# Attention's q, k, v projection with tokens on the partitions, in a two-layer trunk on one core

## What is computed

```python
qkv = (xn @ w_qkv).reshape(B, S, 3, N_HEADS, HEAD_DIM).astype(jnp.float32)   # 512 tokens, 16 heads of 64
q = rmsnorm(qkv[:, :, 0], g_q)          # mean square over the 64 channels of a head, per token
k = rmsnorm(qkv[:, :, 1], g_k)
v = qkv[:, :, 2]
for window, dil in DILATED_PAIRS:       # (128,1), (512,4), (2048,16), merged by their denominators
    o, m, den = dilated_branch(q, k, v, rel_table, window, dil)
...
return o.reshape(B, S, D).astype(xn.dtype) @ w_o
```

## Time and profile before

| | |
|---|---|
| median of three runs | 1132.68 us |
| the profiled execution, and its span | 1132.44 us, 1130.6 us |
| granted TensorE clock, mean | 1.000 |
| busy: PE, DVE, ACT, POOL | 99%, 51%, 43%, 41% |
| attention's stages, first matmul to the last | 504.15 to 711.47 us |
| its tail, to the last head's outputs | 711.47 to 741.62 us |

### The profile page before, as it was taken

One profiled execution on the slowest core, in us unless ns is written; L12 is line 12 of the kernel. 1 busy time (PEld: TensorE's weight loads), 2 busy tenths in 40 slices (PEclk: granted clock), 3 DMA queues, 4 the chain that ended last, 5 costly groups with the idle time before them and its releaser, 6 DMA issues.

```text
span 1130.6 us, 16046 instructions
## 1 busy us (share of the span) xinstructions
PE 1124.8 (99%) x5228; PEld 936.7 (83%) x5228; DVE 582.0 (51%) x1047; ACT 487.7 (43%) x750; POOL 461.7 (41%) x221
## 2 busy tenths in 40 slices
PE   9999999999999999999999999999999999999998
PEld 7788888888888888888888888878888888888887
DVE  6875754545445412225777777777844545450000
ACT  5333444444444432324666666644534444341220
POOL 4454534354443445443223332134544344434442
PEclk9999999999999999999999999999999999999999
DMA  8232322322322233332322223122332222223331
GB/s 267 83 106 93 112 77 95 107 93 93 110 78 92 63 108 98 102 109 70 92 75 74 74 88 100 64 75 93 112 111 90 96 95 90 95 63 104 100 100 76
DMA packets 38925, 108.11 MB, mean 96 GB/s; under 512 B 4272, under 2 KB 7344, under 8 KB 38896
## 3 DMA queue, kind: packets, MB, share of 16 engines
q1 hardware_dynamic: 36560, 103.49, 28.7%
q10 hardware_dynamic: 2336, 4.24, 1.3%
HBM read 105.57 MB, written 2.15 MB: 95 GB/s over the span
## 4 chain that ended last, share of the span: by engine, by line
issue 45%; PE 33%; POOL 20%; DMA 1%; POOLq 0%; SPq 0%; ACT 0%; DVE 0%; DVEq 0%
POOL wl L431 20%; PE bank L1087 7%; PE bank L1086 7%; PE bank L1085 7%; PE spt L1085 4%; PE spt L1086 4%; PE spt L1087 4%; DMA raw<-w_in 1%; SPq L361 0%; POOLq L430 0%; POOLq L436 0%; PE obank L1087 0%; PE obank L1086 0%; PE obank L1085 0%; SPq L368 0%
## 5 line engine op out<-in xcount | busy, mean ns | idle before, releaser
L431 POOL TENSOR_TENSOR wl<-raw,wh 128x1024 fp32r<-128x1024 f32 (+2 forms) x214 | 457.5, 2144 | 644.2 <-ACT wh L466 644.2
L1085 PE MATMUL bank<-xh,wh 128*128 128x512 f32 x992 | 390.5, 394 | 0.0
L1087 PE MATMUL bank<-xh,wl 128*128 128x512 f32 x992 | 386.6, 390 | 0.0
L1086 PE MATMUL bank<-xl,wh 128*128 128x512 f32 x992 | 386.2, 389 | 0.0
L466 ACT ACTIVATE wh<-raw 128x1024 fp32r<-128x1024 f32 (+2 forms) x214 | 201.3, 945 | 145.1 <-PE spt L1087 139.4
L1087 PEld LDWEIGHTS bank<-xh,wl 128*128 128x128 f32 x992 | 186.2, 188 | 39.2
L1086 PEld LDWEIGHTS bank<-xl,wh 128*128 128x128 f32 x992 | 186.4, 188 | 37.4
L1085 PEld LDWEIGHTS bank<-xh,wh 128*128 128x128 f32 x992 | 186.3, 188 | 37.2 <-issue 0.4
L908 DVE TENSOR_TENSOR work<-bank,rstd 128x512 f32<-128x512 f32 x88 | 60.6, 691 | 225.0 <-PE bank L1087 223.1
L1085 PE MATMUL spt<-bh,wh 128*128 128x512 f32 x440 | 171.5, 390 | 0.4 <-POOL wl L431 0.3
L1086 PE MATMUL spt<-bl,wh 128*128 128x512 f32 x440 | 171.2, 389 | 0.0
(11 more groups left out here) (155 smaller groups left out, 938.3 us busy)
## 6 DMA issues: line engine op xcount, KB each, us to landing
raw<-w_up SPq DMA_DIRECT2D x88, 512.0 KB, 3.2
raw<-w_down SPq DMA_DIRECT2D x32, 384.0 KB, 3.1
raw<-w_down SPq DMA_DIRECT2D x32, 320.0 KB, 2.9
raw<-w_qkv SPq DMA_DIRECT2D x16, 512.0 KB, 3.6
raw<-w_in SPq DMA_DIRECT2D x14, 512.0 KB, 4.2
raw<-w_out SPq DMA_DIRECT2D x8, 512.0 KB, 3.2
raw<-w_qkv SPq DMA_DIRECT2D x16, 256.0 KB, 2.8
work<-bias_rows ACTq DMA_DIRECT2D x16, 256.0 KB, 3.1
```

Source lines behind the costliest of these rows:

```text
L431: nc.gpsimd.tensor_tensor(wl[s][:, 0:n], raw[s][:, 0:n], plain(wh[s][:, 0:n]), ALU.subtract).then_inc(s_lo, 1)
L1085: mm(dst, wh[s][:, w], hi, start=first, stop=False)
L1086: mm(dst, wh[s][:, w], lo, start=False, stop=False)
L1087: return mm(dst, wl[s][:, w], hi, start=False, stop=last)
```

## The change

The activations become stationary and the weights move. A pair's q, k and v come out together, tokens on the partitions, in blocks of 128 tokens: `token_product` writes 384 columns (128 of each of q, k, v). Four blocks of tokens by 8 slices of channels by three matmuls make 96 matmuls of 384 columns where there were 72 of 512. They go in two passes over the weights, blocks 0 and 1, then 2 and 3, and use banks 0 and 1 both times (pair 0: banks 0 to 3). A unit holds two slices of channels (768 columns, QKV = 4 x 768), and is released in the second pass.

ScalarE takes each block out of PSUM in three operations (`evacuate`); VectorE adds up squares along the free dimension (`sums`), makes the factors (`norm_factors`, twelve linked small operations), and multiplies q and k by them in place (`normalise`). v needs no turning. Instead q and k are turned, 4 transposes each (`turn`), into banks 2 and 3, from where ScalarE rounds them and VectorE takes the rests. The norm's factor of x isn't spread any more (it scales v by token, and cancels in q's and k's norm up to the epsilon, which is scaled). All stages are unrolled, the first activation of ScalarE (to load its table early) is gone, and the tail is in another order.

TensorE and the units:

```diff
-QKV = (SLOT, SLOT, SLOT // 2, SLOT // 2)
+QKV = (6 * P,) * RING
...
-            def qkv_part(p, which, s, k0, k1, at=0):
-                for k in range(k0, k1):
-                    last = product(bank[which][:], s, k - at, xh[:, k, :], xl[:, k, :], k == 0, k == KT - 1)
...
+            def token_product(b, t, k):
+                dst = bank[b][:, 0:3 * P].rearrange("q (w n) -> q w n", w=3)
+                rows = slice(t * P, (t + 1) * P)
+                mm(dst, xh[:, k, rows], pair_weights(wh, k), start=k == 0, stop=False)
+                mm(dst, xh[:, k, rows], pair_weights(wl, k), start=False, stop=False)
+                return mm(dst, xl[:, k, rows], pair_weights(wh, k), start=False, stop=k == KT - 1)
...
+            def turn(pair, which):
+                if which:
+                    pe.wait_ge(s_kn, pair + 1)
+                    pe.wait_ge(s_kl, 2 * pair)
+                else:
+                    pe.wait_ge(s_qn, pair + 1)
+                    pe.wait_ge(s_ql, 2 * pair)
...
+                for t in range(TB):
+                    at = t * 2 * P + which * P
+                    last = nc.tensor.transpose((qbank, kbank)[which][:, t * P:(t + 1) * P],
+                                               qk[pair % 2][:, at:at + P], ident)
...
+            def stage(p):
+                mid, old = p >= 1, p >= 2
+                if old:
+                    score_blocks(p - 2, 1)
+                tokens(p, 0, 0, 5)
+                if mid:
+                    turn(p - 1, 1)
+                tokens(p, 0, 5, 6)
+                if old:
+                    transposes(2 * (p - 2) + 1)
+                tokens_end(p, 0)
+                if p == 0:
+                    norm_stats(2)
+                if mid:
+                    turn(p - 1, 0)
+                if old:
+                    outputs(p - 2, 1)
+                tokens(p, 1, 0, 2)
+                if mid:
+                    score_blocks(p - 1, 0)
+                tokens(p, 1, 2, 6)
+                if mid:
+                    transposes(2 * (p - 1))
+                tokens_end(p, 1)
+                if mid:
+                    outputs(p - 1, 0)
```

TensorE's tail:

```diff
-            wo_part(0, 0, 5)
-            transposes(2 * end - 1)
-            wo_part(0, 5, 6)
-            wo_part(1, 0, 3)
-            score_blocks(2 * end, 0, 1)
-            outputs(end - 1, 1, 0)
-            turn_v(end)
...
+            score_blocks(end - 1, 1)
+            pe.wait_ge(s_vl, TB * PAIRS)
+            wo_part(0, 0, 6)
+            wo_part(1, 0, 3)
+            turn(end, 1)
+            transposes(2 * end - 1)
+            wo_part(1, 3, 5)
+            outputs(end - 1, 1)
+            turn(end, 0)
+            wo_part(1, 5, 6)
+            pe.wait_ge(s_kept, 2)
+            for n in range(2):
+                wo_part(n, 6, 7)
+            score_blocks(end, 0)
```

ScalarE:

```diff
+            def evacuate(pair, t):
...
+                nc.scalar.activation(qk[pair % 2][:, at], bank[b][:, 0:2 * P], ACT.Copy).then_inc(s_qc, 1)
+                if pair:
+                    act.wait_ge(s_kn, pair)
+                nc.scalar.activation(qksq[:, at], bank[b][:, 0:2 * P], ACT.Square).then_inc(s_qs, 1)
...
+                nc.scalar.activation(v_heads(pair, t, lo=False), v_part(b), ACT.Copy,
+                                     scale=small[:, 3, t:t + 1]).then_inc(s_vh, 1)
```

VectorE:

```diff
+            def normalise(pair, which):
+                dve.wait_ge(s_qc, (pair + 1) * TB)
+                view = heads_of(qk[pair % 2], which)
+                nc.vector.tensor_tensor(view, view, factors(1, which), ALU.mult).then_inc((s_qn, s_kn)[which], 1)
...
```

## The result

The changed kernel takes 1167.27 us (median of 4, 1166.44 to 1169.62), the kernel before 1132.63 us on the same chip: ratio 1.031, interval 1.0298 to 1.0323. It is slower by 34.6 us. The forecast was 1162, with 1150 to 1170 as the likeliest case's range and 1122 to 1169 as the range of 80%.

A forecast was written before the change was run, and what follows sets the result against it. TensorE was taken to bind (busy 99%), with each head's chain hidden before. Stages +17.2 us and tail +12.4 gave +29.6 on 1132.44: 1162 us, likeliest case's range 1150 to 1170, range of 80% 1122 to 1169.

The forecast's parts named there:

- likeliest case: GpSimd's units delay divisions and norm factors in the stages, and the tail waits: 1162 us, chance .42.
- TensorE alone: Attention stages counted by TensorE's work without waits: net -2.2 us per pair, stage 24.65 us, eight pairs 17.6 us less.
- the forecast's own terms: TensorE's work per pair: 3.15 us of operations gone, .94 added for two turns, .06 more for the matmuls.
- The norm's block: GpSimd's unit 3 holds the norm factors in each steady stage; TensorE waits 1.25 us before turn k.
- The tail: End of the attention: waits summing to 11.7 us, 5.4 of them for head 13's output; 42.6 us, +12.4.
- signs of being wrong: Divisions at 1.27 us for four, TensorE idle under 1 us per stage, matmuls .19 apart, or granted clock under 1.
- the rival with the clock: TensorE's matmuls at 1.2 instead of 2.4 GHz, +.227 us per 512-column matmul; 1165 to 1175, chance .09 shared with weight loads.
- One block only: In the stages GpSimd gets two units in one go or misses one: stage about 27.9 us, 1150, chance .14.
- Order of issue: Four queued divisions go ahead of GpSimd's unit, only norm factors are held: stage 26.15 us, 1136, chance .09.
- TensorE bound throughout: No waits in stages, the tail's waits gone too: -18.6 us, 1114, chance .08.
- Free chain: Head's chain in the stages stays clear of GpSimd: stage 24.85 us, -6.9, 1125, chance .18.
- Weight loads as the bound: A 188 ns load must end before the next starts: 1.7 us per stage, up to +13.5; chance .09 shared with clock.

The follow-up runs named there:

- e1: Changed kernel, with GpSimd's unit 1 waiting from pair 1 on until VectorE's four divisions of head 0 are done: 1138.63 us, ratio to before 1.0056.
- e3: Kernel before the change, with ScalarE rounding the next pair's weight unit 0 ahead of its copy of v: 1138.32 us, ratio 1.0052.
- e2: As e1, and GpSimd takes unit 3 only behind the norm factors as well: 1133.32 us, ratio 1.0009.
- e6: Changed kernel with both gates on GpSimd and the tail's new order, w_o's units also waiting for divisions of heads 13 and 15: 1121.4 us, ratio .9902.
- e5: Changed kernel without gates, only the tail reordered (q turned behind k, w_o's slice kept earlier, last scores before the previous head's outputs): 1157.77 us, ratio 1.022.
- e7: As e6, and ScalarE rounds pair 0's last unit before loading the exponential's table: 1120.16 us, ratio .9892.
- e8: Changed kernel without gates, with ScalarE rounding units 1 and 2 behind the rounding of the transposed probabilities: 1155.34 us, ratio 1.0188.

## Why the prediction was right, point by point

- **Direction, place and mechanism: right.** GpSimd's two units fall into the four divisions. The forecast had TensorE lose 3.6 us there per stage; the transposes take 3.2 longer, of which 2.5 are idle. e1 shows the cause by taking it away, e3 by bringing it into the kernel before.
- **TensorE alone: nearly right.** Without waits a stage is 25.28 us by e2 and 25.26 by e6; forecast 24.65, though the forecast's own terms (3.15 - .94 - .06) give 24.73. About half of the difference is the pace, .1735 against the .1705 misread in the score block, 96 x .003 = .29 us; for the rest I had counted the slow first matmul behind each removed group as saved, while the new order has as many changes between groups. That this is all of it isn't shown. Over eight stages the saving is 207.3 - 193.6 = 13.7 us (e6, with 2.1 us of waits in its stages), not 17.6.
- **The norm's block: the right place, too large.** L772 is held for 1.72 us (forecast 1.8), but the wait before turn k is 3.4 us in six stages: 1.31 in the first, .3 to .5 in the others, not 1.25. In the stage shown VectorE ended its factors 4.7 us after the stage's end rather than 5.1, and TensorE came to turn k at 6.7 rather than 6.38.
- **The tail: right.** The wait for head 13's output is 5.36 us (forecast 5.4), the tail 43.05 (42.6). e5 shows that it is of the order.
- **What was left out: the clock.** A fall was only a rival, tied to the tail's wait, and a granted clock under 1 stood among the signs of being wrong; it was .990. It fell behind the waits in five of the seven stages too: 28.85 us a stage at full clock, 30.4 otherwise. The step that failed is the sum's assumption that a wait of 1.2 us costs 1.2 us. In the stages, 47 matmuls of 384 columns start mostly .32 us apart instead of .174, 7 us together, and the six behind the wait of 5.4 us take 2.70 (752.41 to 755.11) instead of 1.36. These 8 us are more than the 5.3 between forecast and result; TensorE's own work (+.6 a stage) and smaller waits (about -.4 and, before turn k, -.8 a stage) together make a stage at full clock .65 us shorter than forecast (28.85 against 29.5). So 1162 lies this close to 1167 partly by luck, by two errors of opposite sign, and the measured time is also inside the 1165 to 1175 that the rival with the clock was given.
- **The rivals.** One block only, 1150: out, the four divisions take 4.40 to 5.48 us in all seven stages. Order of issue, with all queued divisions first: out by e3. TensorE bound throughout: out by the waits. Free chain, 1125: out for this kernel, though e6 and e7 reach that state with gates and another tail, 1121 and 1120; its point of decision (a rounding more than about .6 us later) was too simple, for in e8 rounding comes much later and the units then hold up the norm. Weight loads as the bound: out, .1735 is under .188. Of such a lock the Trainium skill ("SBUF — State Buffer", section "Who interferes with whom") says: "Whoever issues first gets the shared pair for the whole instruction". That a held instruction waits for a whole one of the other engine, the trace shows (the second division 2.05 us, .41 alone). But the sentence is about one instruction; that four queued divisions would all go first was my reading of it, and e3 and this trace show GpSimd getting in between them.

## What to carry to other kernels

An engine that is idle half of the time can still set the pace: look at when it asks for something shared, not at how busy it is. A change that takes an instruction out of a third engine's queue moves that moment; here a copy of v that was dropped on ScalarE had kept GpSimd off VectorE's divisions. Where two engines exclude each other, one semaphore that lets the background one start right behind the critical operations was worth 29 us here, while reordering alone moved the collision.

## What the runs showed of the hardware

GpSimd's subtractions and VectorE's divisions in SBUF take turns, instruction by instruction: with four of VectorE's queued, two units went in between (4.46 us for 1.27 of work). The norm's operations of 16 columns on SBUF were held too (1.72 us where .17 is usual), as was a sum of two SBUF tiles (2.06 us at 415.85, .69 alone). VectorE's operations that read PSUM ran at .68 us beside a unit (in the kernel before at 646.52 us), and so did a reduction of one SBUF tile (.69 at 632.85 of e8). Waits of 1.3 and 1.2 us on TensorE, .55 us apart, were followed in three stages by 3.4 us at the 1.2 GHz level (granted clock .94 over such a stage; 636.1 to 639.5 in the one shown), and in two others with the same waits by none (1.00); which condition decides isn't settled by these runs. Three runs of 128 columns as a moving operand take as long as one of 384.
